# The sample columns of the layer 0 convolution, moved from VectorE to GpSimd

## What is computed

```
u = h @ w_in
a_val, a_gate, a_g, c_q, kv, b_g = split(u)
glu = a_val * sigmoid(a_gate)
ext = concatenate([conv_hist, glu], axis=1)      # 30 old steps ahead
y[t, c] = b[c] + sum over k < 31 of w[k, c] * ext[t + k, c]
ya = silu(layernorm(y))
```

## Time and profile before

| what | value |
|---|---|
| median of three runs | 3165.96 us (3163.75 to 3166.63) |
| profiled execution, its own time | 3167.61 us |
| span of its instructions | 3165.8 us |
| PE busy | 2744.4 us, 87% |
| DVE busy | 1502.2 us, 47% |
| ACT busy | 940.4 us, 30% |
| POOL busy | 517.3 us, 16% |
| mean granted clock of PE | 0.931 of full |

### The profile page before, as it was taken

The page is one execution under the profiler, slowest core; times in us unless marked ns, Lnnn a source line. Parts: engine busy times, 40 slices in busy tenths (PEclk is TensorE's granted clock), DMA queues, the critical chain, the costliest instruction groups (busy, mean ns, idle before and its releaser), DMA issues. The chain is left out here.

```text
span 3165.8 us, 43537 instructions
## 1 busy us (share of the span) xinstructions
PE 2744.4 (87%) x17210; PEld 2233.1 (71%) x17210; DVE 1502.2 (47%) x2592; ACT 940.4 (30%) x1749; POOL 517.3 (16%) x372
## 2 busy tenths in 40 slices
PE   5997867887997989988979999987789898699789
PEld 4997654555666879856779999975455553699566
DVE  3999734664554320145455562124677672300352
ACT  3222333451222222222223222225353531322221
POOL 2221320002330322102212112110000000221011
PEclk8998888998997989999989999985899998899899
DMA  2311460006440012223032222359546350122141
GB/s 83 101 47 39 144 206 24 1 1 222 172 176 21 1 34 74 87 82 131 1 80 86 89 94 82 93 153 285 127 92 146 73 91 0 47 74 87 53 167 49
DMA packets 284489, 286.18 MB, mean 90 GB/s; under 512 B 48182, under 2 KB 236310, under 8 KB 279651
## 3 DMA queue, kind: packets, MB, share of 16 engines
q1 hardware_dynamic: 264898, 195.52, 22.2%
q0 software_dynamic: 13696, 67.11, 5.9%
q10 hardware_dynamic: 5760, 21.63, 1.7%
HBM read 239.19 MB, written 45.47 MB: 90 GB/s over the span
## 5 line engine op out<-in xcount | busy, mean ns | idle before, releaser
L307 PE MATMUL pp<-HH,WS_part 128*128 128x352 f32 x2208 | 715.6, 324 | 0.0
L305 PE MATMUL pp<-HH,WH 128*128 128x352 f32 x1728 | 564.1, 326 | 31.1 <-POOL WS_part L454 31.1
L306 PE MATMUL pp<-HT_part,WH 128*128 128x352 f32 x1728 | 558.5, 323 | 0.0
L307 PEld LDWEIGHTS pp<-HH,WS_part 128*128 128x128 f32 x2208 | 417.8, 189 | 0.0
L305 PEld LDWEIGHTS pp<-HH,WH 128*128 128x128 f32 x1728 | 327.7, 190 | 32.8 <-POOL WS_part L454 32.6
L306 PEld LDWEIGHTS pp<-HT_part,WH 128*128 128x128 f32 x1728 | 327.4, 189 | 0.0
L454 POOL TENSOR_TENSOR WS_part<-WS,WH 128x1024 fp32r<-128x1024 f32 x72 | 180.3, 2504 | 672.0 <-ACT WH L401 672.0
L2644 PE MATMUL OP<-oWO,YT 128*128 128x512 f32 (+1 forms) x576 | 257.2, 603 | 16.3 <-DVE XE L2776 16.3
L826 DVE SCALAR_TENSOR_TENSOR CV<-GX,cw,CV x360 | 215.8, 677 | 0.0
L2644 PEld LDWEIGHTS OP<-oWO,YT 128*128 128x128 f32 (+1 forms) x576 | 104.4, 184 | 156.0 <-issue 137.6
L1986 DVE TENSOR_REDUCE xmx<-xS 128x4 f32<-128x1024 f32 x16 | 19.5, 1219 | 375.9 <-PE xS L1947 375.9
(11 more groups left out here) (483 smaller groups left out, 4917.2 us busy)
## 6 DMA issues: line engine op xcount, KB each, us to landing
WS<-o_w_in SPq DMA_DIRECT2D x40, 512.0 KB, 3.9
WS<-x_w_qg SPq DMA_DIRECT2D x32, 512.0 KB, 4.0
HT<-cache_mem_k SPq DMA_DIRECT2D x16, 1024.0 KB, 8.1
HT<-cache_mem_v POOLq DMA_DIRECT2D x16, 1024.0 KB, 8.5
CBt<-cum_scratch SPq DMA_DIRECT2D x8, 2048.0 KB, 10.4
xbc_scratch<-oACC ACTq DMA_DIRECT2D x24, 528.0 KB, 2.7
XT<-xbc_scratch SPq DMA_DIRECT2D x8, 1536.0 KB, 13.3
WS<-e_w_in SPq DMA_DIRECT2D x20, 512.0 KB, 4.0
```

Source lines behind the costliest of these rows:

```text
L305: nc.tensor.matmul(out, wh, xh, start=start, stop=False)
L306: nc.tensor.matmul(out, wh, xl, start=False, stop=False)
L307: return nc.tensor.matmul(out, wl, xh, start=False, stop=stop)
```

## The change

DVE no longer touches the 32 sample columns. POOL does them, for all four channel tiles in one instruction: 128 elements for each partition, as [4 tiles, 8 sequences, 4 steps]. The sum of a tap takes two instructions there: a product into one of two new small buffers, and an add onto `CV`. `project` gets a hook, `gpsimd_each`, which is called on POOL behind the low part of every block. The hook returns at once for the first two jobs (blocks 0 to 15). Behind the low part of block 16 it waits for the last values and gates, multiplies them for the sample, writes the bias into the sums, and does taps 0 to 7; behind block 17 taps 8 to 15, behind block 18 taps 16 to 23, behind block 19 taps 24 to 30. So POOL gets 1 + 1 + 31 + 31 = 64 instructions more. The product of the next tap is issued ahead of each add. Everything else is as it was.

```diff
--- before.py
+++ after.py
@@ -453,6 +453,8 @@
                         pool.wait_ge(p_hi, n0 + k + 1 + j * blocks)
                         nc.gpsimd.tensor_tensor(WL[:, k % slots, :, :], WS[:, k % slots, :, :], WH[k % 2][:, :, :],
                                                 ALU.subtract).then_inc(p_lo, 1)
+                        if "gpsimd_each" in extra:
+                            extra["gpsimd_each"](pool, plan.index(n0), k)
             if "gpsimd" in extra:
                 extra["gpsimd"](pool)
 
@@ -803,8 +805,6 @@
 
                 for parity in range(2):
                     dve.wait_ge(p_ev[parity], 3 * (n2 + 1) + ct * 3)
-                new = GXS[:, ct, :, HIST:HIST + TS]
-                nc.vector.tensor_tensor(new, new, CV[:, ct, TP:TOK].rearrange("p (b t) -> p b t", b=NB), ALU.mult)
                 dve_own.enter(ct, 2 * CK + 1)
                 new = GXP[:, ct, HIST:HIST + TP]
                 dve_own.step(dve, nc.vector.tensor_tensor(new, new, CV[:, ct, 0:TP], ALU.mult))
@@ -812,8 +812,7 @@
                 for k in range(CK):
 
                     first = [(CV[:, ct, 0:half], GXP[:, ct, k:k + half])]
-                    rest = [(CV[:, ct, half:TP], GXP[:, ct, k + half:k + TP]),
-                            (CV[:, ct, TP:TOK].rearrange("p (b t) -> p b t", b=NB), GXS[:, ct, :, k:k + TS])]
+                    rest = [(CV[:, ct, half:TP], GXP[:, ct, k + half:k + TP])]
                     for parts in (first, rest):
                         if k:
 
@@ -828,9 +827,40 @@
                         dve_own.did(ins)
                 dve_own.leave(4)
 
+        acc = CV[:, :, TP:TOK].rearrange("p c (b t) -> p c b t", b=NB)
+        prod = [sb(c, f"sprod{a}", [P, 4, NB, TS]) for a in range(2)]
+        shape = [P, 4, NB, TS]
+
+        def sample_conv(pool, part, k):
+
+            if part < 2:
+                return
+            turn, V = 2 * (part - 2) + k, nc.gpsimd
+            if turn == 0:
+                for parity in range(2):
+                    pool.wait_ge(p_ev[parity], 3 * (n2 + 4))
+                new = GXS[:, :, :, HIST:HIST + TS]
+                pool_own.step(pool, V.tensor_tensor(new, new, acc, ALU.mult))
+                pool_own.step(pool, V.tensor_copy(acc, cb[:].unsqueeze(2).unsqueeze(3).to_broadcast(shape)))
+
+            def product(tap):
+                w = cw[:, :, tap:tap + 1].unsqueeze(3).to_broadcast(shape)
+                pool_own.did(V.tensor_tensor(prod[tap % 2][:], GXS[:, :, :, tap:tap + TS], w, ALU.mult))
+
+            first, end = 8 * turn, min(8 * turn + 8, CK)
+            product(first)
+            for tap in range(first, end):
+                if tap + 1 < end:
+                    product(tap + 1)
+                    pool.wait_ge(pool_own.sem, pool_own.value() - 1)
+                else:
+                    pool_own.wait(pool)
+                pool_own.step(pool, V.tensor_tensor(acc, acc, prod[tap % 2][:], ALU.add))
+
         project(c, [(glu_col, 2, 4, glu, None), (gate_col, 2, 4, gates, None), (query_col, 1, 2, queries, None),
                     (kv_col, 1, 2, keys, None)],
-                HT, HH, 2, {"vector": convolve, "sync_first": memory_loads, "scalar": memory_squares, "gpsimd": memory_rstd},
+                HT, HH, 2, {"vector": convolve, "sync_first": memory_loads, "scalar": memory_squares, "gpsimd": memory_rstd,
+                          "gpsimd_each": sample_conv},
 
                 [split_part(CK2, [P, KT, P], at=a * D) for a in range(2)])
 
```

## The result

The changed kernel takes 3247.43 us (median of four, 3244.9 to 3248.72) against 3166.3 before (3163.75 to 3166.79). The ratio is 1.0257, interval 1.0239 to 1.0275. The forecast of 3171.5 and its range, 3152 to 3195, were both far too low. The mechanism is that of rival D, starvation, to which I had given 0.14; the price that I had put on D was 3282.

A forecast was written before the change was run, and what follows sets the result against it. DVE's convolution ended the stage, 12.1 us behind ACT. DVE would lose 20.7 us and regain 18.3, but PE's stalls on POOL would start `front` 5.5 us later: 3165.96 + 5.5 = 3171.5 us, range 3152 to 3195.

The forecast's parts named there:

- rival D: POOL starves between DVE's halves, gets in only between tiles, and PE waits: 116 us slower, 3282; chance 0.14.
- What that costs DVE: In DVE's convolution, 63 small POOL instructions cost 0.29 us each, 18.3 us together; DVE ends at 303.5.
- What POOL's work costs PE: Blocks 17 to 19: POOL's turns delay low parts, PE stalls and ends at 305.5; `front` starts 5.5 us later.
- C: In the convolution, POOL gets in behind every second half only: 22 us slower, 3188; chance 0.20.
- the likeliest case: The forecast itself: POOL gets in behind every half of the convolution; 3171.5 us, chance 0.36.
- a pure gain of 20.7 us: Short sample instructions leaving DVE's convolution save 20.7 us; alone this would end DVE at 285.2.
- The exclusion: In the convolution, POOL's instruction and DVE's two-input one don't run side by side; a low part costs DVE 2.19 us.
- The price of a cold restart: When PE restarts after stopping, about 4 us run at half clock speed, losing 2 us.
- stops of 4 to 5 us: PE's stalls ahead of blocks 17 to 19 may cost clock; half a restart, 1.1 us, put on the last block.
- Rival A: POOL's small instructions slip into the convolution without slowing DVE: 12.1 us faster, 3153.9; chance 0.18.
- Rival B: POOL's product and add go back to back, one DVE half between pairs: -3 to +4 us; chance 0.12.

The follow-up runs named there:

- experiment 4: The whole change, with DVE's second half cut in 480 and 32 columns, against the kernel before: 3173.57 us, ratio 1.0032.
- p2_quarters: The changed kernel without any sample work, DVE's second half cut in two quarters of 256 columns, the last without a wait: 3312.76 us.

## Why the prediction was wrong

**The step that failed** is the assumption on which "What that costs DVE" and "What POOL's work costs PE" both stand: "If it gets in behind every half, one instruction goes through for each 0.66 + 0.29 = 0.95 us. I take that." POOL does not get in behind a half: its low parts were passed by up to 43 halves. So the sum lacked its largest term. It had PE wait for low parts 17 to 19 only, and nothing for blocks 3 to 15; the waits of blocks 4, 6, 8 and 10 came to 85.7 us. The rows had said it: ten boundaries between halves passed over, one used. I wrote that down under C and D and still gave the likeliest case the opposite. The one exception lay at the start of a tile, behind the fourth instruction from a pause of DVE. The large DVE instruction of the earlier trace rows that spoke against D was the fourth of four behind a pause too (3.19 us idle before the first, at 1009.35). So neither spoke for a boundary in the middle of a long run, and D should have been the likeliest.

**A second error** follows. I costed the removal as a pure gain of 20.7 us. The sample's instruction did a second job, opening DVE's run for POOL once a tap, and I named that only in rival D.

**What held.** DVE ended the stage before, and its own instructions take less by about what I had said: a tile's run is 39.84 us, against 49.02 - 2 x 2.19 = 44.64 before without its two low parts, 4.80 a tile and 19.2 for four, where I had 19.5. The exclusion is real: a low part costs DVE 2.1 to 2.2 us wherever it gets in (41.99 - 39.84 after the change, 3.56 - 1.42 with the pause). One of POOL's instructions with two inputs of 128 elements takes 0.41 to 0.47 us beside an idle DVE; the forecast had 0.47. The price of a cold restart, 2 us, fits the 9.0 us of four.

The rest of the sum was not tested by the changed kernel, where the 64 instructions ran beside an idle DVE. With the door open (experiment 4) it can be compared, though not as the same kernel: there DVE has one instruction more in each tap, and its run of a tile is 54.72 - 5 x 2.19 = 43.77 us, 3.9 longer. The forecast had low part 17 ready at 257.0, the run 262.4; low part 18 at 274.9, 279.1; low part 19 at 292.8, 295.8; one instruction for each 0.95 us, 0.91 in the last tile and 1.5 to 1.75 in the third; `front` 5.5 us later, 10.0. DVE's loss for each was forecast at 0.29 and measured at 0.18. DVE ended at 313.0 and not at 303.5, and ACT's chain ended the stage, as forecast. That both come out as small losses is in part luck. I had left open whether stops of 4 to 5 us cost clock, and put 1.1 us on one; two stops of about 3 us did, the one read above at 1.7. For DVE's loss the Trainium skill ("SBUF — State Buffer", section "Who interferes with whom") has the one that issues first hold the ports for its whole instruction. Worked out from that, the loss would be 0.46 us for each, an estimate; the measured 0.18 does not agree.

**Rival A** is refuted for an open door: small instructions do not slip in, they take up to 1.75 us. **Rival B** did not occur: product and add lie 0.9 us apart with DVE's work in between. **Rival C** describes the third tile of experiment 4 only. **Rival D** had the mechanism. It had one low part for each tile, DVE itself held up between tiles, and the end at 422; two get through, since DVE's pause at the head of a tile lets one in and the next one follows behind it. The stage ended at 387.5. `p2_quarters` shows D's course as I had drawn it, one low part for each tile and DVE idle for 16 to 17 us ahead of the next, with 152.6 us of waits and its stage ending at 452.4.

## What to carry to other kernels

Before you take a small instruction off a busy engine, ask what happens at its two boundaries, not only what it costs: here 19.5 us of short instructions held a door open that was worth 81. Where POOL stands on PE's path and DVE runs two-input instructions back to back, look at which of DVE's boundaries the waits of POOL's instructions end, and how far each lies behind a pause; one exception in eleven is not a rule. To take work off DVE beside a working POOL, try ACT first: of the two places tried here it is the one that gained.

## What the runs showed of the hardware

POOL's instruction with two inputs does not take the first free moment. Behind DVE's running two-input instructions of 128 to 512 columns its record, 2.4 us of which is its own work, lasted up to 31.7 us with halves, passed by 43 of them, and up to 44.4 us with quarters, passed by 86. It waited no longer than a tap when a piece of 32 or 64 columns, or a pause of 0.27 us, lay in every tap. DVE's starts are 0.16 us apart behind 32 columns, 0.20 behind 64, and 0.26 behind 128, which do not open it. Shortly behind a pause of DVE it is let in between two long instructions too: behind the fourth in the kernel before (at 257.57), behind the fifth with halves; behind the seventh it was refused. The Trainium skill ("SBUF — State Buffer", section "Who interferes with whom") has the one that issues first hold the shared ports for the whole instruction, and the other wait until it finishes. That they exclude each other agrees with the 2.1 to 2.2 us for which DVE stands at a low part of 2.37. That the other waits only until the one in hand has finished does not: by these runs a waiting POOL instruction can be passed by dozens that came later. The cause in the hardware stays open: neither the wait ahead of an instruction, nor the signal behind the one before, nor the pattern decides, and why 64 columns open and 128 do not, no run here tells. That an empty instruction doesn't open it, that a completed wait does, and that it shuts only some instructions behind a pause, speaks for DVE having to run dry, but that was not measured by itself. Not tried were pieces between 64 and 128 columns, and a run with only one input each.
